# Expert layers of a two-block model: two of four token tiles through streamed expert tables and a gate table, two through gathered rows

## What is computed

```python
q = (xb @ w_q).reshape(T, PEER_HEADS, 2, PEER_HALF)          # 8 heads, 2 halves of 128
s = einsum('thpd,hpkd->thpk', q, sub_keys)                   # 128 scores for each half
sv, si = top_k(s, 16)                                        # of each half
cand = sv[:, :, 0, :, None] + sv[:, :, 1, None, :]           # 16 x 16 sums
top_s, pos = top_k(cand, 16)
eidx = (si[0] * 128 + si[1])[pos]                            # 16 of 16,384 experts
gate = softmax(top_s)
u = expert_u[eidx];  act = gelu(einsum('thkd,td->thk', u, xb))
v = expert_v[eidx];  y = einsum('thk,thkd->td', gate * act, v)
```

## Time and profile before

| | |
|---|---|
| time, median of 3 runs | 3460.39 us (3454.99 to 3462.05) |
| span of the profiled execution | 3459.0 us |
| busy: PE, DVE, ACT, POOL | 1958.3, 2003.2, 674.6, 2070.7 us |
| moved by DMA | 1167.08 MB, mean 337 GB/s |
| mean granted TensorE clock | 0.736 |

### The profile page before, as it was taken

The page is one execution under the profiler, slowest core; times in us unless marked ns, Lnnn a source line. Parts: engine busy times, 40 slices in busy tenths (PEclk is TensorE's granted clock), DMA queues, the critical chain, the costliest instruction groups (busy, mean ns, idle before and its releaser), DMA issues.

```text
span 3459.0 us, 30792 instructions
## 1 busy us (share of the span) xinstructions
PE 1958.3 (57%) x10149; PEld 1019.7 (29%) x10149; DVE 2003.2 (58%) x4999; ACT 674.6 (20%) x1905; POOL 2070.7 (60%) x2099
## 2 busy tenths in 40 slices
PE   8998997444444444434279684544445444343675
PEld 3554654222222222212034352222222222221221
DVE  1243427777777777766511157777777777676210
ACT  3011213111121121111131112121211111111231
POOL 1313214777777777766665226777777777677573
PEclk9999788666566666665689797666666666656798
DMA  6223146999999999999998759999999999999995
GB/s 234 73 73 110 49 158 244 410 409 409 409 400 409 409 405 405 402 409 401 377 366 288 265 188 351 409 409 409 409 409 406 403 409 403 405 399 408 351 393 220
DMA packets 338224, 1167.08 MB, mean 337 GB/s; under 512 B 37114, under 2 KB 40468, under 8 KB 336916
## 3 DMA queue, kind: packets, MB, share of 16 engines
q0 software_dynamic: 294912, 1073.87, 79.1%
q1 hardware_dynamic: 43156, 91.26, 7.2%
HBM read 1162.90 MB, written 2.10 MB: 337 GB/s over the span
## 4 chain that ended last, share of the span: by engine, by line
DMA 31%; POOL 25%; PE 19%; issue 10%; DVE 8%; ACT 1%; POOLq 0%; DVEq 0%; ACTq 0%
PE banks L778 16%; DMA scr<-in_peer_down,idx 14%; DMA scr<-in_expert_u,idx 14%; POOL ring L729 12%; POOL scr L717 12%; DVE scr L2080 5%; PE banks L1125 3%; DMA ring<-in_expert_v,idx_v 1%; DMA scr<-in_expert_v,idx_v 1%; POOL scr L729 1%; DMA const<-in_peer_up,idx_v 1%; DMA ring<-in_peer_up,idx_v 1%; ACT hT L1348 0%; DVE ring L2048 0%; DVE ring L2045 0%
## 5 line engine op out<-in xcount | busy, mean ns | idle before, releaser
L2080 DVE CUSTOM_DVE_ANT_0 scr<-scr,banks 128x1024 f32<-128x1024 f32 x1024 | 1223.8, 1219 | 575.3 <-DMA scr<-in_peer_down,idx 281.6
L1125 PE MATMUL banks<-ring 128*32 128x512 f32 x3712 | 675.3, 864 | 1167.0 <-DMA ring<-in_peer_up,idx_v 551.9
L717 POOL DMA_INDIRECT scr<-in_expert_u,idx x512 | 488.0, 953 | 324.5 <-DVE scr L2080 126.9
L717 POOL DMA_INDIRECT scr<-in_peer_down,idx x512 | 487.0, 951 | 264.2 <-DVE scr L2080 124.0
L1125 PEld LDWEIGHTS banks<-ring 128*32 128x32 f32 x3712 | 136.4, 138 | 1546.1 <-issue 1460.5
L729 POOL DMA_INDIRECT ring<-in_peer_up,idx_v x464 | 436.8, 941 | 179.4 <-issue 144.0
L729 POOL DMA_INDIRECT ring<-in_expert_v,idx_v x464 | 436.6, 941 | 162.1 <-issue 144.8
L778 PE MATMUL banks<-ring,scr 128*128 128x128 f32 (+1 forms) x2112 | 393.7, 368 | 4.6 <-ACT ring L1498 4.6
L778 PEld LDWEIGHTS banks<-ring,scr 128*128 128x128 f32 x2112 | 366.5, 271 | 23.4 <-issue 19.2
L689 POOL TENSOR_TENSOR ring<-ring,silu 128x4096 f32<-128x4096 f32 x8 | 56.2, 7022 | 312.5 <-DMA ring<-in_w_mod 312.5
L778 PE MATMUL banks<-ring,hT 128*128 128x512 f32 x512 | 234.7, 618 | 14.6 <-DVE X L1976 11.8
(11 more groups left out here) (232 smaller groups left out, 2214.5 us busy)
## 6 DMA issues: line engine op xcount, KB each, us to landing
ring<-in_w_mod SPq DMA_DIRECT2D x12, 2048.0 KB, 8.0
ring<-in_w_in SPq DMA_DIRECT2D x7, 2048.0 KB, 12.8
scr<-in_peer_w_q SPq DMA_DIRECT2D x1, 8192.0 KB, 28.0
scr<-in_peer_down,idx POOLq DMA_INDIRECT x512
scr<-in_w_q SPq DMA_DIRECT2D x4, 2048.0 KB, 7.9
scr<-in_expert_u,idx POOLq DMA_INDIRECT x512
ring<-in_peer_up,idx_v POOLq DMA_INDIRECT x464, 11.2
ring<-in_expert_v,idx_v POOLq DMA_INDIRECT x464, 11.2
```

What stands on the lines that cost most here:

```text
L717: nc.gpsimd.indirect_dma_start(u_rows[:, k % SLOTS, :], None, table_u, bass.IndirectOffsetOnAxis(idx[:, n % IDX_SLOTS, k:k + 1], 0)).then_ ...
L1125: last = nc.tensor.matmul(psum[2 + c][32 * g:32 * g + 32, :], spread[:, n % 2, k, :], up_rows[slot + g][:, c * CW:(c + 1) * CW], start=(h ...
L2080: V.tensor_tensor_reduce(u_rows[:, k % SLOTS, :], u_rows[:, k % SLOTS, :], xn, 1.0, 0.0, ALU.mult, ALU.add, dots[:, n % 2, k:k + 1]).then_ ...
```

## The change

Tiles 0 and 1 (`DENSE = 2`) no longer gather. Instead all 128 chunks of 128 experts of both tables pass through PE for 256 tokens at once:

- **Gate table.** For each token the 128 picks (head, rank) have a first key i1 and a second key i2, both 0 to 127, and a gate. DVE (`picks_b`) compares a ramp with i1 and i2 and so makes `pick_a` and `pick_b`, each 128 picks x 16 tokens x 128; POOL (`picks_a`) multiplies `pick_a` with the gates; PE (`gate_table`) multiplies both for each token, which gives its gates for all 16,384 experts; ACT copies them out and SP writes them to memory, `gates_out` (16.8 MB a layer). This is done 16 times a layer, for 16 tokens each.
- **Streaming.** For chunk c, PE transposes the 128 down rows (`turned`), multiplies them with the 256 tokens (`hidden_of`, 8 matmuls of 256 columns), ACT takes the gelu, DVE multiplies with the gate table (`weigh`), and PE adds gelu x gate x up rows onto the four PSUM banks that hold the outputs of tiles 0 and 1 (`add_up`, 4 matmuls of 512 columns). `hidden_of` runs 9 chunks ahead.
- **Rows.** Tiles 2 and 3 (16 heads) still gather, 256 down and 256 up rows-of-128 a layer. The dot product now reads the tokens from SBUF (`xn_last`), and the up rows lie as the down rows do, one token a partition, so that DVE scales and sums them itself (`row_op`).

The layer becomes two stages in each engine's program: `routing` (25 steps; 24 of the 32 heads are routed, the gate table is made, 9 chunks are hidden already), and `dense` (128 steps, one chunk each, with about 4 row operations a step; the last 7 heads are routed inside it). The queries of two tiles are one job (matmuls of 256 columns). The work that stood beside the old layer now stands behind it; the opening of each layer does no gathers.

```diff
+DENSE = 2
+DW = DENSE * P
+LEAD = 9
+DN_SLOTS = 3
+UP_SLOTS = 4
+ROW_SLOTS = 8
+N_STEPS = 3 * PH + 1
+HIDDEN_STEPS = (8, 9, 10, 11, 12, 21, 22, 23, 24)
+LATE_ROUTES = {3: 25, 7: 26, 11: 27, 15: 28, 19: 29, 23: 30, 27: 31}
...
+def rows_upto(u):
+
+    return min(N_ROWS, -(-N_ROWS * (u + 1) // (NKEYS - 2)))
...
+            def dense(layer):
+                for slot in range(2):
+                    sp.wait_ge(spilled[slot], 16 * (N_BATCH // 2) * (layer + 1))
+                for g in range(2):
+                    load_gates(layer, g)
+                for c in range(UP_SLOTS):
+                    load_up(layer, c)
+                for u in range(NKEYS):
+                    c = u + LEAD
+                    if c + 1 < NKEYS:
+                        next_down(layer, c + 1)
...
+                    if u + UP_SLOTS < NKEYS:
+                        sp.wait_ge(up_done, layer * NKEYS + u + 1)
+                        load_up(layer, u + UP_SLOTS)
...
+                pool.wait_ge(a_found, layer * N_BATCH + m + 1)
+                nc.gpsimd.tensor_tensor(pick_a, pick_a, pick_keys[:, 2, tok].unsqueeze(2).to_broadcast([P, 16, P]), ALU.mult
+                                        ).then_inc(a_set, 1)
...
+                        if n >= ROW_SLOTS:
+                            pool.wait_ge(row_used, layer * N_ROWS + n - ROW_SLOTS + 1)
...
+            def hidden_of(layer, c, turn_next):
+
+                if turn_next:
+                    turned(layer, c + 1, 0)
+                empty(pe, "T", layer, c, 1)
+                o = take("H", layer, c)
+                for k in range(KT):
+                    if turn_next and k == 4:
+                        turned(layer, c + 1, 1)
+                    last = mm(o[:, 0:DW], dT[:, c % 2, k, :], hT[:, k, 0:DW], k, KT)
...
+            def gate_table(layer, m):
+
+                pe.wait_ge(a_set, layer * N_BATCH + m + 1)
+                pe.wait_ge(b_set, layer * N_BATCH + m + 1)
+                for j in range(4):
+                    o = begin("G", layer, m, j)
+                    for q in range(4):
+                        last = mm(o[:, q * P:(q + 1) * P], pick_b[:, 4 * j + q, :], pick_a[:, 4 * j + q, :], 0, 1)
+                    last.then_inc(bank_ready, 1)
...
+            def add_up(layer, c):
+
+                n = layer * NKEYS + c
+                pe.wait_ge(weighted, n + 1)
+                pe.wait_ge(up_in[n % UP_SLOTS], 16 * (n // UP_SLOTS + 1))
...
+            def picks_b(layer, m):
+
+                b = m % PH
+                if b == 0:
+                    empty(dve, "KT", layer, m // PH)
+                if m > 0:
+                    full(dve, "G", layer, m - 1, 3)
+                V.tensor_tensor(pick_a, iota.unsqueeze(1).to_broadcast([P, 16, P]),
...
+                    V.tensor_tensor_reduce(rows[slot], rows[slot], xn_last[h // PH], 1.0, 0.0, ALU.mult, ALU.add, dots[:, h, k:k + 1]
+                                           ).then_inc(row_used, 1)
...
+                    V.scalar_tensor_tensor(row_sum[k % 2], rows[slot], weight[:, h, k:k + 1], row_sum[k % 2], ALU.mult, ALU.add
+                                           ).then_inc(row_used, 1)
```

More of the change, by code:

```diff
@@ L95, with dots_step, hidden_in_step @@
 for _n in range(2):
[L96 to L131, removed]
+    CHUNK_LAST_JOB.update({("w_mod", CW * (4 + _n)): ("g1", _n), ("w_mod", CW * (10 + _n)): ("g2", _n)})
+def rows_upto(u):
+    return min(N_ROWS, -(-N_ROWS * (u + 1) // (NKEYS - 2)))
+def dots_step(h):
+    done = TOPK * (ROW_HEADS.index(("D", h)) + 1)
+    return next(u for u in range(NKEYS) if rows_upto(u) >= done)
+def hidden_in_step(i):
+    return [c for c, step in enumerate(HIDDEN_STEPS) if step == i]
 def chunk_number(name, col=0):
@@ new lines, in dense @@
+    def dense(layer):
+        for u in range(NKEYS):
+            if u in LATE_SCORES:
+                jobs.add(("s", layer, LATE_SCORES[u]), "A", 4)
+            if u + LEAD < NKEYS:
+                hidden_of(layer, u + LEAD)
+            if layer == 1 and u >= NKEYS - 2:
+                jobs.add(("pT", u - (NKEYS - 2)), "A", 4 + 2 * (u - (NKEYS - 2)))
+    open_layer(0, "wo", "n1")
+    routing(0)
+    dense(0)
+    for t, bank in ((2, 4), (3, 6), (0, 0), (1, 2)):
+        tile("gm", t, (bank, bank + 1))
@@ L764, in _ @@
+            gathers(1)
         @block.tensor
@@ new lines, in dense @@
+            def dense(layer):
+                for u in range(NKEYS):
+                    if u in LATE_SCORES:
+                        scores(layer, LATE_SCORES[u])
+                    c = u + LEAD
+                    if c < NKEYS:
+                        hidden_of(layer, c, c + 1 < NKEYS)
+                    if layer == 1 and u >= NKEYS - 2:
+                        p_cols(u - (NKEYS - 2))
+                    if u == 0:
+                        drained(range(2 * DENSE))
+                    add_up(layer, u)
@@ new lines, in _ @@
+            queries(0, 0)
+            project("wo", 3, w)
+            empty(pe, "kT", 0, 3)
+            scores(0, 0)
+            queries(0, 1)
+            tile_rows("n1", 2)
+            scores(0, 1)
+            queries(0, 2)
+            tile_rows("n1", 3)
+            for half in range(2):
+                turned(0, 0, half)
+            for half in range(2):
+                empty(pe, "nt", "n1", 3, half)
+            routing(0)
+            dense(0)
+            for t in (2, 3, 0, 1):
+                tile_rows("gm", t)
@@ new lines, in routing @@
+            def routing(layer):
+                for i in range(N_STEPS):
+                    t, h = divmod(i, PH)
+                    if i == DENSE * PH + PH:
+                        keys_of(layer, DENSE, 0)
+                    if i > 0:
+                        route(layer, i)
+                    if h == PH - 1:
+                        softmax_shift(layer, t)
+                    if h % 2 == 1 and t < DENSE:
+                        keys_of(layer, t, h // 2)
+                    if h == 0 and t > 0:
+                        softmax(layer, t - 1)
+                    if i > PH:
+                        picks_b(layer, i - PH - 1)
```

1680 lines of the change are left out of this document (799 added, 881 removed).

## The result

The changed kernel takes 3557.16 us (median of 3 runs, 3553.97 to 3560.57) where the kernel before takes 3460.39: a ratio of 1.0277, 95% interval 1.0263 to 1.0291, so 97 us slower. Run again later in this study, both on one chip, the ratio was 1.0277 [1.026, 1.0294].

The account below looks back on a forecast made before the run. The prediction took DMA traffic, nearly all gathers, to bound the kernel. 476.5 + 99 + 296 + 1034 + 245 + 296 + 1034 + 97 gave 3577.5 us of span, so 3579 us was forecast; 8 in 10 range 3440 to 3725.

Parts of the forecast that it names:

- Opening: Start of layer one, before routing: matmuls, norms, keys, first transposes and waits, 99 us; 92 in layer two.
- middle: From the end of layer one's dense stage through layer two's opening: chain 33, column jobs 111, opening 92; 245 us.
- Tail: Behind layer two's dense stage: gate matmuls, norms and the end of the kernel, 97 us.
- Routing: Stage before gathers can start in each layer: 296 us, bounds 240 and 330.
- plain step: One of routing's 16 pick steps: two comparisons, POOL's multiply, PE's products and hand-overs in a row, 12.7 us.
- two hand-overs of the key tables: In routing, softmax, transposes and copies of the key tables: 16 us a layer.
- Dense: Streaming stage of each layer, bound by bytes at 993 us plus start and waits: 1034 us, bounds 1006 and 1110.
- Rate: In the dense stages, plain loads mixed with gathers move at the earlier trace's 408 GB/s.
- the streams disturb each other: Rival, dense stage: late chunks and rows idle DMA and PE, stage 1105 us, total 3721 us; 20%.
- The comparison runs beside POOL: Rival, pick steps: second comparison overlaps POOL's multiply, 10.4 us a step, routing 266 us, total 3519 us; 15%.
- Routing costs only DVE's own time: Rival, 16 pick steps: 9.4 us each, routing 240 us, total 3467 or 3411 us; 12% faster, 3% about equal.
- the ring: In each pick step, comparisons, multiply, products and the next comparison wait for one another in turn; priced 12.7 us.

Follow-up runs that it names:

- e1: Changed kernel with the two pick comparisons in swapped order, so that the one POOL waits for comes second; 3568.48 us, ratio 1.0306.
- e5: Changed kernel loading only the first half of each up row and using it twice (another output), on the third chip; 3442.43 us.
- e3: Changed kernel with two pairs of pick buffers, so that comparisons wait for the products of the batch before last; 3509.57 us, ratio 1.0133.
- e8: Changed kernel with two pairs of pick buffers and ACT's softmax exponential ahead of the hidden columns, on the third chip; 3503.43 us.
- e11: Changed kernel with two pairs of pick buffers, the exponential ahead of the hidden columns, and ACT instead of POOL multiplying the gates; 3648.92 us, ratio 1.0552.
- e4: Changed kernel with ACT doing the softmax's exponential ahead of the step's hidden columns; 3550.18 us, ratio 1.0252.
- e6: Changed kernel with hidden products computed over half of the features (another output), on the third chip; 3559.92 us.

## Why the prediction held

Predicted were 3579 us, measured 3557: the time came out of the mechanism of the sum, 22 us below it (25 in the profiled span, 3552.2 for 3577.5).

- *Opening* 99: measured 95.7, at clock 0.98. The *middle* 245: measured 235.2, of which the chain 32.2 for 33 and the columns 110 for 111; the second opening is 86.7 for 92. *Tail* 97: measured 98.0.
- *Routing* 296: measured 301.0 and 300.8, with parts that err both ways, so that 296 came this near is in part luck: 16 steps at 11.95 us are 12 us less than written, and the rest of the stage 17 more. A plain step is 11.95 us for 12.7: the hand-overs are short, and PE's products take 3.90 us for 4.2. The two hand-overs of the key tables and the steps with hidden chunks take more: DVE waited 16.2 us a layer for the exponentials alone. What held is the step on which the rivals turned, that comparison, comparison, multiply and products stand in a row: e1 shows the multiply at 3.61 us by itself and 5.59 beside a comparison. I had POOL start when the second comparison ends; the trace starts its record earlier and has the wait inside it, with the same end. The Trainium skill ("SBUF — State Buffer", SBUF: two separate sides) has the lock held by whichever engine starts first, with the other waiting: here both sides of it are seen, POOL's multiply longer by 2.0 us and DVE's sum by 1.47.
- *Dense* 1034: measured 1020.3 and 1024.7. The start is 20.8 and 21.0 for 16, and PE's first sums wait 15.3 us for an up chunk. The body is 999.5 and 1003.7 us, for 993 by the bytes and 25 that I had added for last rows and for PE and DMA waiting in turn. Those 25 are the term that was mis-sized, at some 8. PE's floor of 975 us was near as well: when e5 makes PE the limit, the sums of a layer take 956 us from first to last. `weigh` (L2148) takes 0.62 us for the 0.43 priced, which costs nothing: DVE is busy 758.6 us of the stage, for 765.
- *Rate*: 406 GB/s in both stages, gathers and plain loads mixed, as the 408 of the earlier trace rows. By the figure of the Trainium skill that the prediction quoted against it ("DMA: Bandwidth & Descriptors", Specifications, some 358 GB/s) the stage would take 1131 us; the trace, of a kernel on one core, disagrees with it again.

Of the rivals, *the streams disturb each other* is out: 1020 us and not 1105, though DVE's idle time still ends mostly on rows that landed late (226.1 and 257.8 us above). *The comparison runs beside POOL* is out by e1. (Its 266 us for routing don't follow from 10.4 us a step, which would give 259; nothing rests on it.) *Routing costs only DVE's own time* was the right alarm, since it is what e3 and e8 make of the stage: with the ring gone a plain step is 10.78 us and routing ends 25 us earlier, at some 276 us and not at the rival's 240. The 9.4 us that I gave it come near what DVE does alone (9.31 us between two comparisons of e11 with no wait, 775.18 to 784.49), but as long as POOL multiplies, L2049 adds its 1.47 us.

Where did the expected gain go? The bytes of a layer fell from 537 MB to some 436 by the prediction's count (gathers 268, tables 134, gates 17 written and 17 read), and its transfer-bound time from 1316 us to 1000. In return 301 us of routing, 96 and 87 of openings and 149 between the layers lie bare. Of this only 49 us at the first opening and 75 between the layers were without gathers before. No version with the whole computation that was measured on a chip like the first is faster than the kernel before; e3 comes nearest, 48 us above it. e8's 3503 us, measured on the third chip, are 43 us above the 3460 of the other two.

## What to carry to other kernels

Halving the traffic of a transfer-bound stage pays only for what stays beside it: price the stage that must now run before the transfers can start, and the work that the old transfers covered. In a loop over several engines look for the ring first: a second buffer (48 us here) was worth more than any change of who does the work, and moving work to an idle engine cost 94 to 145 us, since that engine's place in the order closed a longer ring. A vector TENSOR_TENSOR with both inputs in SBUF and a GpSimd tensor instruction there add up, and the wait can stand inside the record of either; MAX8, which has one such input, ran beside POOL at its usual time.

## What was not expected of the hardware

- The kernel before took 3461.8 us (7 runs, 3458.3 to 3467.1) on one chip, 3460.1 on another, and 4039.3 (7 runs, 4028.8 to 4052.3) on a third, 17% more. Its mean granted clock there was 0.71, on the first chip 0.74. The versions made from the changed kernel seem to take no longer there: e8 3503.4 us, 6 below e3 on the first chip, where the same extra edit (e4) was worth 7; and e6 3559.9. On that chip the change is a gain (e8 to before: 0.8676 [0.8645, 0.8706]). What is slow there is not settled: no trace of the kernel before was taken on it. Since it is the kernel with twice the gathers that suffers, I suspect the gathers; the runs don't show it, and e6's dense stage speaks against it: on that chip it moved 406 GB/s, two thirds of it gathers, as on the first.
- Issuing a gather takes POOL 1.19 to 1.28 us on the mean (L805) beside DVE's row instructions, which now read two SBUF operands; it took 0.95. The shortest still take 0.93, the longest 2.87. That they wait for DVE's row instructions is likely, but no run tests it. With 512 a layer it stays hidden.
- Waiting PE is granted less clock: in e6, busy 246 of 300 us, it is 0.94, and the sums L1210 take 656 ns in place of 607; this cost nothing, as bytes were the limit.
